# Differential attention of prompt and sample in one phase: a prompt head and a sample stream side by side in eight slots

## What is computed

```
def diff_attend(q, q_pos, k, v, k_pos, lam):
    s = jnp.einsum('bqhmd,bkhmd->bhmqk', q, k) * (A_HEAD_DIM ** -0.5)
    mask = (k_pos[None, :] // CHUNK) <= (q_pos[:, None] // CHUNK)
    p = jax.nn.softmax(jnp.where(mask, s, NEG), axis=-1)
    w = p[:, :, 0] - lam * p[:, :, 1]
    return jnp.einsum('bhqk,bkhe->bqhe', w, v)
...
        h = h + mix                                              # mix = o @ w_o_a
        h = h + sq_relu_mlp(rmsnorm(h, norm_mlp[l]), w_up[l], w_down[l])
```

## Time and profile before

| | |
|---|---|
| three runs | 3875.07, 3881.35 (median), 3894.73 us |
| profiled execution, first to last instruction | 3875.0 us, as good as the fastest run |
| busy share of the span | PE 90%, PEld 77%, DVE 43%, ACT 28%, POOL 12% |
| "pa" and "da" together | from 353.5 to 876.7 us of the span |

### The profile page before, as it was taken

One profiled execution on the slowest core, in us unless ns is written; L12 is line 12 of the kernel. 1 busy time (PEld: TensorE's weight loads), 2 busy tenths in 40 slices (PEclk: granted clock), 3 DMA queues, 4 the chain that ended last, 5 costly groups with the idle time before them and its releaser, 6 DMA issues. The chain is left out here.

```text
span 3875.0 us, 59511 instructions
## 1 busy us (share of the span) xinstructions
PE 3483.5 (90%) x22994; PEld 2992.9 (77%) x22994; DVE 1676.6 (43%) x2828; ACT 1099.1 (28%) x2118; POOL 478.8 (12%) x188
## 2 busy tenths in 40 slices
PE   6998887886799999999799978877978799999998
PEld 5886776765699999999588767765656799999997
DVE  4432886545444444444212156643432344444445
ACT  3001664433211111222202046642332221121112
POOL 2110000002011111111211000000001111111110
PEclk9998998998899999999799989988998899999999
DMA  4223443972111111110212143427762111111111
GB/s 141 90 81 85 93 92 112 337 289 89 60 38 38 43 43 43 43 43 11 72 61 90 52 95 77 84 61 231 276 229 71 49 43 43 43 43 43 43 43 49
DMA packets 284887, 345.93 MB, mean 89 GB/s; under 512 B 155136, under 2 KB 204448, under 8 KB 284768
## 3 DMA queue, kind: packets, MB, share of 16 engines
q1 hardware_dynamic: 262352, 296.18, 24.7%
q10 hardware_dynamic: 20128, 39.93, 2.9%
q0 software_dynamic: 2304, 8.39, 0.7%
HBM read 300.46 MB, written 43.98 MB: 89 GB/s over the span
## 5 line engine op out<-in xcount | busy, mean ns | idle before, releaser
L772 DVE TENSOR_TENSOR h_rows<-h_rows,m_dn 128x512 f32<-128x512 f32 x576 | 391.4, 686 | 325.4 <-PE m_dn L346 325.4
L344 PE MATMUL m_dn<-m_dn_hi,m_hid_hi 128*128 128x512 f32 x1152 | 449.4, 390 | 0.0
L345 PE MATMUL m_dn<-m_dn_lo,m_hid_hi 128*128 128x512 f32 x1152 | 448.4, 389 | 0.0
L346 PE MATMUL m_dn<-m_dn_hi,m_hid_lo 128*128 128x512 f32 x1152 | 448.2, 389 | 0.0
L756 DVE TENSOR_TENSOR m_relu<-m_relu 128x384 f32<-128x384 f32 x192 | 157.3, 819 | 515.2 <-ACT m_relu L737 515.2
L344 PE MATMUL m_up<-b_xt_hi,m_up_hi 128*128 128x384 f32 x768 | 261.7, 341 | 17.1 <-POOL m_up_lo L677 17.1
L344 PE MATMUL m_up<-c_xt_hi,m_up_hi 128*128 128x384 f32 x768 | 262.0, 341 | 15.1 <-POOL m_up_lo L677 15.1
L677 POOL TENSOR_TENSOR m_up_lo<-m_up_raw,m_up_hi 128x2048 fp32r<-128x2048 f32 x32 | 147.6, 4614 | 931.4 <-ACT m_up_hi L727 931.4
L346 PE MATMUL m_up<-c_xt_hi,m_up_lo 128*128 128x384 f32 x768 | 259.6, 338 | 0.0
L345 PE MATMUL m_up<-c_xt_lo,m_up_hi 128*128 128x384 f32 x768 | 259.6, 338 | 0.0
L345 PE MATMUL m_up<-b_xt_lo,m_up_hi 128*128 128x384 f32 x768 | 259.4, 338 | 0.0
(11 more groups left out here) (328 smaller groups left out, 6943.2 us busy)
## 6 DMA issues: line engine op xcount, KB each, us to landing
da_k_tiles<-in_cache_a_k SPq DMA_DIRECT2D x64, 512.0 KB, 5.8
da_v_tiles<-in_cache_a_v SPq DMA_DIRECT2D x64, 512.0 KB, 5.2
m_up_raw<-in_w_up SPq DMA_DIRECT2D x32, 1024.0 KB, 5.3
m_dn_raw<-in_w_down SPq DMA_DIRECT2D x32, 1024.0 KB, 4.8
db_k_tiles<-in_cache_b_k SPq DMA_DIRECT2D x64, 512.0 KB, 4.9
db_v_tiles<-in_cache_b_v SPq DMA_DIRECT2D x64, 512.0 KB, 4.9
qkv_w_raw<-in_w_qkv_a SPq DMA_DIRECT2D x24, 512.0 KB, 4.0
pa_k_dup<-out_ak_p SPq DMA_DIRECT2D x32, 256.0 KB, 4.4
```

Source lines behind the costliest of these rows:

```text
L344: pe.matmul(out, lh, rh, start=start, stop=False)
L345: pe.matmul(out, lh, rl, start=False, stop=False)
L346: return pe.matmul(out, ll, rh, start=False, stop=stop)
L772: dve.tensor_tensor(hc, hc, dns[n % 3][:], ALU.add).then_inc(s_de, 1)
```

## The change

`pa` and `da` are replaced by one phase, `joint_attention` "ja". It has nine slots (`for i in range(HEADS + 1)`), each of eight steps s. In slot i the prompt head i runs beside the scores of stream i and the values of stream i-1; slot 8 holds only the values of stream 7. The loops are written out in full. PSUM is divided anew: `ja_s0` and `ja_s1` two banks each, one bank for the prompt's outputs, one for the samples', and **two** banks `ja_t0` and `ja_t1` that serve every other product in turn: kq units, weights, key tiles, sample scores, sample probabilities and selections. A unit may be written when the unit two places before it in TensorE's order has been copied out. The two copies of a pair of score tiles become one of 512 columns. The store of a head's output moves from POOL's queue to SP's.

`h_rows` is given up after "qkv" and allocated again; "oa" loads the nine rows anew (`reload`), each behind one of its weight pieces on SP's queue.

```
+    def residual_rows(self, ctx, tag):
+        self.h = ctx.enter_context(self.nc.sbuf_tensor(f"{tag}_h_rows", [P, RT, D], F32))
...
+            if reload:
+                core.load_row(sp, 0)
+                core.load_row(sp, 1)
             for n in range(2, PARTS * len(pieces)):
                 load(n)
...
+                if reload:
+                    core.load_row(sp, n)
+            if reload:
+                core.load_row(sp, RT - 1)
...
+                    if reload and dst == 0:
+                        dve.wait_ge(core.s_row[r], 32)
                     dve.tensor_tensor(hc, hc, src_, ALU.add).then_inc(s_ev, 1)
...
+        def kq_of(s):
+            return (s,) if s < 6 else (6, 7) if s == 6 else ()
...
+        KEYS = ((0,), (1,), (2,), (3,), (4,), (5,), (6, 7), ())
+        SCORES = ((), (), (0,), (), (1,), (), (2,), (3, 4))
+        PROBS = ((), (), (0,), (1,), (2,), (3,), (4,), ())
+        VALUES = ((), (), (), (0, 1), (2, 3), (4, 5), (6, 7), (8,))
...
+            def fill(key):
+                n = unit[key] = len(unit)
+                if n >= 2:
+                    pe.wait_ge(s_te[n % 2], n // 2)
+                return TB[n % 2]
...
+            for i in range(HEADS + 1):                     # TensorE
+                prompt, bs, bv = i < HEADS, i, i - 1
+                for s in range(QT):
+                    g = QT * i + s
+                    ahead = prompt and g + 1 < QT * HEADS
+                    if ahead:
+                        scores(g + 1, 0)
+                    if prompt and i + 1 < HEADS and kq_of(s):
+                        kq_unit(i + 1, kq_of(s)[0])
+                    if bs < STREAMS:
+                        for u in SCORES[s]:
+                            d_scores(bs, u)
+                        for t in KEYS[s]:
+                            d_keys(bs, t)
+                    if ahead:
+                        scores(g + 1, 1)
+                    if prompt and i + 1 < HEADS and s == 6:
+                        kq_unit(i + 1, 7)
+                    if 0 < g <= QT * HEADS:
+                        values(g - 1)
+                    if prompt:
+                        weights(g)
+                    if s == 1 and bv >= 1:
+                        d_select(bv - 1)
+                    if bv >= 0:
+                        for t in VALUES[s]:
+                            d_values(bv, t)
+                        for u in PROBS[s]:
+                            d_probs(bv, u)
...
+                for s in range(QT):                        # VectorE
+                    if s == 0 and bv >= 0:
+                        d_maximum(bv)
+                    if prompt:
+                        combine(g)
+                    if ahead:
+                        maximum(g + 1, 0)
+                    if prompt and i + 1 < HEADS and kq_of(s):
+                        kq_low(i + 1, kq_of(s)[0])
+                    if bs < STREAMS:
+                        for u in SCORES[s]:
+                            d_scores_out(bs, u)
+                            d_partial_maximum(bs, u)
+                        for t in KEYS[s]:
+                            d_keys_out(bs, t)
+                    if prompt and i + 1 < HEADS and s == 6:
+                        kq_low(i + 1, 7)
+                    if ahead:
+                        maximum(g + 1, 1)
+                    if 0 < g <= QT * HEADS:
+                        outputs(g - 1)
+                    if s == 1 and bv >= 1:
+                        d_selected(bv - 1)
+                    if s == 2 and bv >= 0:
+                        d_coefficients(bv)
+                    if bv >= 0:
+                        for u in PROBS[s]:
+                            if u % 2 == 0:
+                                d_probs_out(bv, u)
...
-        prompt_attention(nc, core, "pa", False, q, kv["ak_p"], kv["av_p"], None, None, ao)
-        decode_attention(nc, core, "da", False, q[SEQ:ROWS, :], kv["ak_s"], kv["av_s"], cak, cav, None, None, None, ao)
+        joint_attention(nc, core, "ja", q, kv["ak_p"], kv["av_p"], kv["ak_s"], kv["av_s"], cak, cav, ao)
+        core.residual_rows(ctx, "r")
```

More of the change, by code:

```diff
@@ L89, in __init__ @@
         self.sems += self.s_row
-        self.h = ctx.enter_context(nc.sbuf_tensor("h_rows", [P, RT, D], F32))
         self.const = ctx.enter_context(nc.sbuf_tensor("const_sb", [P, NCONST], F32))
@@ L346, in product, with dense_phase @@
     return pe.matmul(out, ll, rh, start=False, stop=stop)
-def dense_phase(nc, core, tag, kind, gain, src, pieces, forget=None, following=None, swap=None):
+def dense_phase(nc, core, tag, kind, gain, src, pieces, forget=None, following=None, swap=None, reload=False):
     with ExitStack() as ctx:
@@ L1640, in stream_step @@
         core = Core(nc, ctx, a["head_sel"], xp, xs)
-        start_phase(nc, core, a["const"],
-                    [a[n] for n in ("lambda_q1", "lambda_k1", "lambda_q2", "lambda_k2")])
         wa = a["w_qkv_a"].rearrange("n d e -> (n d) e")
         with ExitStack() as rows:
+            core.residual_rows(rows, "x")
+            start_phase(nc, core, a["const"],
+                        [a[n] for n in ("lambda_q1", "lambda_k1", "lambda_q2", "lambda_k2")])
             core.normed_rows(rows, "a")
@@ L1655, in stream_step @@
                         [(a["w_o_a"].rearrange("n d e -> (n d) e"), c, "add", c) for c in (0, HALF)],
-                        following=a["norm_mlp"][0, :])
+                        following=a["norm_mlp"][0, :], reload=True)
             mlp_phase(nc, core, "m0", a["w_up"][0], a["w_down"][0], a["norm_kv"])
```

446 lines of the change are left out of this document (added).

## The result

Before: 3875.97 us median of 20 runs (3870.87 to 3894.73). After: 3886.76 (3879.08 to 3904.76, 20 runs). The ratio is 1.0027, with a 95% interval of 1.0019 to 1.0036: 0.27% or some 10.5 us longer, which is inside the half per cent that the prediction called no change. The profiled execution took 3883.78, its span is 3882.1.

The account below looks back on a forecast made before the run. No engine is full; idle time could be filled, but a closed chain across engines sets the slot. Terms 519.2 + 7.0 (clock) + 1.5 (reload) = 527.7 against 523.2 us: 4.5 longer, 3885 us predicted, range 3838 to 3914.

Parts of the forecast that it names:

- The closed chain: Inside a slot, combination through low part, second key unit and second exponential to next combination: 7.4 us a step, 50.0 for eight.
- named signs: New profile: slots of 59 to 65 us, VectorE and ScalarE no busier than summed, TensorE waiting 1 to 3 us for low parts.
- The sum: Start 24.7, head 0 50.0, head 1 58.6, heads 2 to 6 310.5, head 7 50.8, tail 24.6: 519.2 us.
- The reload: Nine rows loaded anew in "oa": 1.5 us taken; as a slower rival up to 23 us, chance 0.08.
- 1.0 us x 7 slots: Step 0 of a slot: a 2.6 us wait lowers the clock, the next score product takes 1.0 longer; 7.0 us in all.
- are like the second and cost nothing: Waits of 1.4 to 1.9 us in steps 2, 3 and 5 resemble a 0.87-busy stretch that kept full clock; cost 0.
- the slow rival: Two or three waits in each full slot bring the half clock: 18 to 27 us, total 3903 to 3912; chance 0.22.
- The delays: VectorE copies ahead of combinations, and TensorE's own work in steps 4 and 6, lengthen a slot's chain: 12.1 us together.
- +3.3: VectorE's copy of the second select unit, at step 1's end, waits for TensorE: 3.3 us more than the chain.
- The probability copies: VectorE's copies at the ends of steps 2, 4 and 6 delay the next combinations by 2.2, 2.4 and 0.8 us.
- The cover: The sample's exponential on ScalarE falls into waits of steps 0 and 1: costs nothing, without cover 2.9 us a slot.
- the idle time is filled: Faster rival: copies and combinations slip past each other, slots near 55 us, total 3828 without the clock's share; chance 0.20.

Follow-up runs that it names:

- e1: Changed kernel with the kq units behind the second score product of their step on TensorE, ScalarE and VectorE: 3852.97 us, ratio 0.9927 to the kernel before.
- e10: e1 with ScalarE's first sample exponential and scaled sample outputs ahead of the prompt's first exponential in step 0: 3830.80 us, ratio 0.9889 to the kernel before.
- e5: Changed kernel with a spare VectorE maximum over 512 columns ahead of each of 56 low parts: 3930.75 us, ratio 1.0129 to the kernel before.
- e6: Changed kernel with the spare VectorE maximum twice in VectorE's waits of step 0, slots 1 to 7: 3885.05 us, ratio 1.0026 to the kernel before.
- e2: Changed kernel with VectorE's select copy moved from step 1's end to behind step 2's first maximum: 3890.89 us, ratio 1.0023 to the kernel before.
- e4: Changed kernel with twelve spare transposes ahead of step 0's second key unit, slots 1 to 7: 3890.10 us, ratio 1.0027 to the kernel before.
- e3: Changed kernel with VectorE's probability copies moved behind the next step's combination and first maximum: 3879.14 us, ratio 0.9992 to the kernel before.
- e11: Changed kernel with only ScalarE's first sample exponential and sample outputs moved ahead of step 0's first prompt exponential: 3886.09 us, ratio 1.0026 to the kernel before.
- e8: e7 with VectorE's probability copies also moved behind the next step's combination and first maximum: 3865.57 us, ratio 0.9965 to the kernel before.
- e7: e1 with no kq unit in step 0, two each in steps 5 and 6: 3853.24 us, ratio 0.9934 to the kernel before.

## Why the prediction was right, step by step

**The closed chain: shown.** ScalarE's second exponentials of the first steps of head 3:

```profile
555.83 1.11 ACT L1990 ACTIVATE ja_probs<-ja_s,ja_neg_max 128x1024 f32<-128x1024 f32 x1 [0.76 <-DVE ja_neg_max L2104]
...
564.39 1.01 ACT L1990 ACTIVATE ja_probs<-ja_s,ja_neg_max 128x896 f32<-128x896 f32 x1 [1.65 <-DVE ja_neg_max L2104]
...
571.14 0.90 ACT L1990 ACTIVATE ja_probs<-ja_s,ja_neg_max 128x768 f32<-128x768 f32 x1 [0.83 <-DVE ja_neg_max L2104]
...
581.41 0.79 ACT L1990 ACTIVATE ja_probs<-ja_s,ja_neg_max 128x640 f32<-128x640 f32 x1 [0.67 <-DVE ja_neg_max L2104]
```

The chain's first step measures 8.56 us from one to the next, against 7.4 and 1.0 for the clock. TensorE's waits are right in size too: 2.54 in step 0 against 2.6, and 1.2, 1.8 and 1.4 in steps 2, 3 and 5 against 1.4 to 1.9. Taking the low part out of the chain gives 39 us (e1), with the one follower that was in its way 54 (e10); putting VectorE's work in costs 40 (e5), in longer waits and in the falls of the clock behind them; a quarter of that work beside the chain costs nothing (e6). Two of the named signs are missed by a little: two slots are over 65 us (65.3), and ScalarE works 33.75 a slot instead of 32.5.

**The sum.** Start 22.05 to the first exponential, against 24.7 (the two score products are through at 21.8). The transposes of the new sample rows do take 2.7 of TensorE, as priced, but the start is no longer than before. They fill a wait of 1.46 us that stood ahead of the first score products, and these run for 2.24 us at a granted clock of 1.00, where they took 4.07 at 0.51. Head 0 with its fall of the clock 51.98 against 50.0 and 1.0. Head 1 61.85 against 58.6 and 1.0. Heads 2 to 6 64.3 on average against 62.1 and 1.0. Head 7 and tail 76.66 against 75.4. The reload 0.1 against 1.5: "oa" before took

```profile
876.72:1036.35 159.63, 123.34 (x576) 101.08 (x576) 89.20 (x127) 49.96 (x90) 21.44 (x8) 0.86 0.17 60
```

and 159.73 after, though DMA engines are 0.25 instead of 0.17 busy there. In all 534.3 against 527.7. The forecast of 4.5 us longer was 6.6 short of the 11.1 of block and reload. That the median came out at 3886.8 against 3885 is luck: the median before is 3876.0 over twenty runs, and 3881 over the three that the prediction had, which hides the difference. By terms, the heads came out 10.7 longer than forecast with the clock's share, the start and the reload 4.1 shorter. What is not luck is that the idle time is not filled: the waits came out as worked out.

**The clock: mechanism right, size too small.** "1.0 us x 7 slots" was one fall a slot. There are ten in seven heads of the traced execution, and slots of one kernel that differ by one fall differ by 1.0 (e10), 1.3 (e2: 64.40 and 65.70) and 1.4 us (e4): an estimate of 10 to 14 us, not 7. (In the changed kernel itself they differ by 1.2 to 2.1. In e6, as long as the changed kernel, the trace has six falls in these heads, so the number differs from one execution to the next.) The sentence that failed is that the shorter waits, those of step 3 among them, "are like the second and cost nothing": falls come behind step 3 too, in four heads of seven. The prediction set against its forecast the section "A second HAM failure mode: psum-queue depth-cycling" of the Trainium skill's page "TensorE: Matmul & The Clock Gate". The trace agrees for the waits of steps 0 and 3 only, and not for all of those: behind waits of 0.5 to 1.5 us in the other steps the clock stays at 1.00, and the slow rival's 18 to 27 us did not come.

**The delays: one cause wrong in part.** The "+3.3" of step 2 is there in size: second exponential to second exponential, the step takes 10.27, where the one before it takes 6.75 with a larger tile. But the place of the copy in VectorE's list is not what holds up its first score product, as e2 shows: TensorE's own values, weights and selections are. How much of the rest of the step the copy costs, e2 leaves open. (The forecast for head 1 takes 3.5 off for this delay and not 3.3; that is 0.2 us.) The probability copies, 5.4 a slot with 2.1 left if moved, gave 14 us of 20 (e3): 1.9 a full slot instead of 3.3.

**The cover: right.** The prediction gave ScalarE's sample exponential no cost because it falls into waits: moving it alone gives nothing (e11). Once the low part is off the chain it does cost: the same move then gives 2.7 a slot (e10 against e1), 1.5 of it waits of TensorE and 1.2 its busy time, with fewer falls. The 2.9 that the prediction names without cover is for both exponentials of a slot, and no run measures it: the move concerns the one of step 0 and the outputs.

**The rivals.** That the idle time is filled did not happen, for the reason that spoke against it, the order of VectorE's list, except in step 2, where TensorE's own list holds; but its slot of 55 is within reach (55.8 in e10), by two moves in the lists. The reload did not bite.

What stays open: why a wait of the same length brings a fall of the clock in one head and not in another, why filling one wait hands the fall to the next (e4), and what the select copy costs by itself (e2).

## What to carry to other kernels

Two jobs side by side gain what their idle times hold only if each engine's list lets one job go on while the other waits; with one ring of shared banks, a copy that is late for one job stops the other's products (L1779 in the changed kernel, L1796 in e2, the key unit in e8). Before merging, follow one step around all engines and ask which link goes back to the same step's start. A wait of an engine shows where it stands, not what would be gained (e2): look at what the next engine is doing meanwhile. And when a wait is removed, go through the work that was priced at nothing because it lay in that wait, since it can be the next bound (e7).

## What the runs showed of the hardware

A slot of 64 us with a granted clock of 0.97 or 0.95 has TensorE waits of 0.5 to 2.5 us in most of its steps and falls to 1.2 GHz in one or two of them. One fall more, with the same idle time, made such a slot 1.4 us longer (e4). The same wait brings a fall in one head and not in another: 2.54 us in step 0 does in heads 1, 2, 3, 4 and 6 and not in head 5, 1.78 us in step 3 does in heads 1, 2, 5 and 6 and not in heads 3 and 4. Filling the wait of step 0 with useless transposes kept the clock at 1.00 there, and in three of five full slots the next wait, in step 1, brought a fall that it had not brought before. "pb", untouched, takes 350.0 us at a granted clock of 0.92 in one kernel and 346.6 at 0.93 in the other.
